# A fourth plain tile ahead of the seven-product tiles, spaced weight loads, and a gated half that stays in PSUM

## The reference

```python
def swiglu_ffn(h, wg, wu, wd):
    return (jax.nn.silu(h @ wg) * (h @ wu)) @ wd
...
    for i in range(DEPTH):
        kind, j = i % N_MIXERS, i // N_MIXERS
        sh1p, sc1p, g1p, sh2p, sc2p, g2p = adaln(c_prompt, ada_w[i], ada_b[i])
...
        xp = layer_norm(ALPHA * xp + g1p * op, ln_mix_g[i], ln_mix_b[i])
...
        fp = swiglu_ffn(xp * (1 + sc2p) + sh2p, ffn_w_gate[i], ffn_w_up[i], ffn_w_down[i])
...
        xp = layer_norm(ALPHA * xp + g2p * fp, ln_ffn_g[i], ln_ffn_b[i])
```

## Time and profile before

| | |
|---|---|
| median of 3 runs | 3110.5 us (3109.71 to 3116.89) |
| the profiled execution | 3103.62 us, span 3101.8 us |
| TensorE busy | 2932.5 us (95%), 21172 matmuls |
| GpSimd, VectorE, ScalarE busy | 56%, 53%, 30% |
| mean granted TensorE clock | 0.98 |

### The profile page before, as it was taken

One profiled execution on the slowest core, in us unless ns is written; L12 is line 12 of the kernel. 1 busy time (PEld: TensorE's weight loads), 2 busy tenths in 40 slices (PEclk: granted clock), 3 DMA queues, 4 the chain that ended last, 5 costly groups with the idle time before them and its releaser, 6 DMA issues.

```text
span 3101.8 us, 53473 instructions
## 1 busy us (share of the span) xinstructions
PE 2932.5 (95%) x21172; PEld 2700.2 (87%) x21172; DVE 1653.5 (53%) x3161; ACT 934.4 (30%) x1825; POOL 1734.0 (56%) x1209
## 2 busy tenths in 40 slices
PE   6999989999999989999989998999999999899997
PEld 4799989999976879999986687999997999899997
DVE  3254684636554774635565547463553536846263
ACT  2220152414220442414234324241422211424141
POOL 2455456857666456767620154676764565468575
PEclk8999999999999999999999999999999999999999
DMA  6643333443345433444321433344422323222332
GB/s 239 224 116 86 119 114 98 136 130 102 99 122 159 151 120 97 162 126 160 94 64 56 115 122 104 109 151 130 157 74 83 102 85 93 62 82 82 87 92 72
DMA packets 450486, 354.85 MB, mean 114 GB/s; under 512 B 26120, under 2 KB 424832, under 8 KB 437933
## 3 DMA queue, kind: packets, MB, share of 16 engines
q1 hardware_dynamic: 435744, 324.79, 34.0%
q10 hardware_dynamic: 14493, 26.63, 2.9%
HBM read 337.86 MB, written 5.25 MB: 111 GB/s over the span
## 4 chain that ended last, share of the span: by engine, by line
PE 76%; DVE 10%; ACT 4%; DMA 2%; issue 2%; DVEq 2%; POOL 1%; ACTq 1%; POOLq 1%; SPq 1%
PE pb L1142 75%; DMA w_raw<-in_ffn_w_up 2%; DMA ada_first<-in_ada_w 1%; DVE part L2727 1%; ACT h_hi L2134 1%; ACT hf L2134 1%; DVE h_lo L2787 1%; DVE xa L2753 1%; DVE pb L2746 1%; DVE hf L2768 0%; DVE h_lo L2777 0%; PE pb L1978 0%; DVE a_lo L2594 0%; POOL a_lo L1048 0%; DVE part L2722 0%
## 5 line engine op out<-in xcount | busy, mean ns | idle before, releaser
L978 POOL TENSOR_SCALAR w_hi<-w_raw 128x1024 fp32r<-128x1024 f32 (+2 forms) x264 | 277.9, 1053 | 714.5 <-DMA w_raw<-in_gmlp_w_in 279.3
L981 POOL TENSOR_TENSOR w_lo<-w_raw,w_hi 128x1024 fp32r<-128x1024 f32 (+2 forms) x264 | 625.8, 2370 | 44.0 <-issue 44.0
L1142 PE MATMUL pb<-a_hi,w_hi 128*128 128x288 f32 x2176 | 601.7, 300 | 33.9 <-POOL w_hi L978 31.9
L1142 PE MATMUL pb<-a_lo,w_hi 128*128 128x288 f32 x2176 | 595.6, 297 | 0.0
L1142 PE MATMUL pb<-h_hi,w_hi 128*128 128x288 f32 x2064 | 548.7, 302 | 47.0 <-DVE pr L2939 19.4
L1142 PE MATMUL pb<-h_lo,w_hi 128*128 128x288 f32 x2064 | 528.7, 297 | 0.0
L1023 POOL TENSOR_TENSOR w_lo<-w_raw,w_hi 128x512 fp32r<-128x512 f32 x304 | 400.8, 1340 | 163.7 <-DVE s_raw L2979 106.6
L1142 PEld LDWEIGHTS pb<-a_hi,w_hi 128*128 128x128 f32 x2176 | 414.2, 190 | 42.1 <-issue 35.5
L1142 PEld LDWEIGHTS pb<-h_hi,w_hi 128*128 128x128 f32 x2064 | 382.8, 191 | 62.3 <-DVE pr L2939 20.4
L1142 PEld LDWEIGHTS pb<-a_lo,w_hi 128*128 128x128 f32 x2176 | 414.7, 191 | 0.7
L1142 PEld LDWEIGHTS pb<-h_lo,w_hi 128*128 128x128 f32 x2064 | 378.7, 191 | 0.0
(11 more groups left out here) (373 smaller groups left out, 4950.5 us busy)
## 6 DMA issues: line engine op xcount, KB each, us to landing
ada_w<-in_ada_w SPq DMA_DIRECT2D x80, 1024.0 KB, 8.9
w_raw<-in_ffn_w_gate SPq DMA_DIRECT2D x88, 512.0 KB, 3.9
w_raw<-in_ffn_w_up SPq DMA_DIRECT2D x88, 512.0 KB, 3.9
w_raw<-in_gmlp_w_in SPq DMA_DIRECT2D x64, 512.0 KB, 4.2
w_raw<-in_ffn_w_down SPq DMA_DIRECT2D x64, 512.0 KB, 5.0
w_raw<-in_gmlp_w_out SPq DMA_DIRECT2D x32, 512.0 KB, 4.9
w_raw<-in_ffn_w_down SPq DMA_DIRECT2D x32, 384.0 KB, 3.7
w_raw<-in_conv_w_pw SPq DMA_DIRECT2D x24, 512.0 KB, 4.2
```

Source lines behind the costliest of these rows:

```text
L978: nc.gpsimd.tensor_scalar(w_hi[:, s, 0:w], w_raw[:, s, 0:w], 1.0, 1.0, ALU.mult, ALU.mult).then_inc(split_hi, 1)
L981: nc.gpsimd.tensor_tensor(w_lo[:, s, 0:w], w_raw[:, s, 0:w], w_hi[:, s, 0:w].bitcast(F32), ALU.subtract).then_inc(split_lo, 1)
L1142: return nc.tensor.matmul(out, lhsT, rhs, start=start, stop=stop)
```

## The change

1. `PAIRED_FROM` goes from 3 to 4: in each layer tile 3 is a plain tile.
2. Loads of conditioning weights are spread (`ada_asked`): one or two more behind a tile instead of four at once, and some between the down projection's units.
3. Slots: after each group's `sums_end` the circle is ordered anew, the slots in the order in which they come free, with the sums' slot third.
4. On GpSimd the first two units of the down weights are split ahead of the last tile's `gated_lower`, and t4 is made ahead of the first paired tile's forms.
5. In the plain tiles (but for the h0 halves of tiles 0 and 1) `gated_in_bank` multiplies in the up product's own PSUM bank and makes both parts from there; only then is that bank given back. Two of them stand ahead of t3 now.
6. In paired tiles the h0 half stays in the bank of p4. ScalarE reads its high part there, VectorE makes its low part (`gated_lower` on VectorE), and gives the bank back. GpSimd makes only the h1 half's.

```diff
-PAIRED_FROM = 3
+GU = ((0, 6), (6, 8), (14, 8))
+PAIRED_FROM = 4
...
+def ada_asked(l, m):
+
+    if m <= 2:
+        return ADA1
+    done = [t for t in ada_groups(l)[0] if t <= m - 2]
+    if not done:
+        return ADA_FIRST + (0, 1, 2, 4)[min(m, 5) - 2]
+    last = max(done)
+    apart = any(last < first <= m for first, _ in GU)
+    return ada_used_by(l, m - 2) + (ADA1 if apart else min(ADA1, m - last))
...
                 self.held[SLOTS - 1] = ("after", (acc_ready, self.products))
+                self.order, self.at = self.pairs[:2] + [SLOTS - 1] + self.pairs[2:], 0
...
                             load_to(plan.mark[l, "m", m])
-                            ada_to(l + 1, ADA1 if m < 4 else ada_used_by(l + 1, m - 3) + ADA1)
+                            ada_to(l + 1, ada_asked(l + 1, m))
                         if n < 2:
+                            load_to(plan.mark[l, "d", n] - 4)
+                            ada_to(l + 1, ada_used_by(l + 1, m) + 2)
+                            load_to(plan.mark[l, "d", n] - 2)
+                            ada_to(l + 1, ada_used_by(l + 1, m) + ADA1)
                             load_to(plan.mark[l, "d", n])
...
             def gated_lower(m):
 
-                for h in (1, 0):
-                    pool.wait_ge(gated_hi, AH.up())
-                    nc.gpsimd.tensor_tensor(one(a_lo, m, half_cols(h)), pr[:, h, :],
-                                            one(a_hi, m, half_cols(h)).bitcast(F32), ALU.subtract
-                                            ).then_inc(a_ready, 1)
+                pool.wait_ge(gated_hi, 2 * AH.up() - 1)
+                nc.gpsimd.tensor_tensor(one(a_lo, m, half_cols(1)), pr[:, 1, :],
+                                        one(a_hi, m, half_cols(1)).bitcast(F32), ALU.subtract).then_inc(a_ready, 1)
...
+                    U.up(2 * len(ms))
+                    split_to(U.n + 2)
                     gated_lower(ms[-1] - GU[n][0])
-                    U.up(2 * len(ms))
...
                 for h in (1, 0):
-                    if h:
-                        act.wait_ge(pair_gated, FQ.n)
-                    else:
-                        act.wait_ge(acc_free, BANKS + G.n)
-                    fn(one(a_hi, m, half_cols(h)), pr[:, h, :], ACT.Copy).then_inc(gated_hi, 1)
+                    act.wait_ge(pair_gated, 2 * FQ.n - h)
+                    src = pr[:, 1, :] if h else pb[:, (G.n - 1) % BANKS, 0:HALF]
+                    fn(one(a_hi, m, half_cols(h)), src, ACT.Copy).then_inc(gated_hi, 1)
...
+            def gated_in_bank(m, h, q):
+                up = pb[:, (G.n + 1) % BANKS, 0:HALF]
+                dve.wait_ge(acc_ready, G.n + 2)
+                dve.wait_ge(sg_ready, SG.up())
+                v.tensor_tensor(up, up, sg[:, q, :], ALU.mult).then_inc(acc_free, 1)
+                dve.drain()
+                v.tensor_copy(one(a_hi, m, half_cols(h)), up)
+                dve.drain()
+                v.tensor_tensor(one(a_lo, m, half_cols(h)), up, one(a_hi, m, half_cols(h)).bitcast(F32),
+                                ALU.subtract)
+                dve.drain().then_inc(a_ready, 1)
+                dve.sem_inc(acc_free, 1)
+                G.up(2)
...
+            def gated_lower(m):
+
+                gated = pb[:, (G.n - 1) % BANKS, 0:HALF]
+                dve.wait_ge(gated_hi, 2 * FQ.n)
+                v.tensor_tensor(one(a_lo, m, half_cols(0)), gated, one(a_hi, m, half_cols(0)).bitcast(F32),
+                                ALU.subtract)
+                dve.drain().then_inc(a_ready, 1)
+                dve.sem_inc(acc_free, 1)
...
                 form_last(l, m)
-                if m != PAIRED_FROM:
-                    dve.wait_ge(a_ready, 8 + a_before(l) + 2 * m)
+                if m != ms[0]:
+                    gated_lower(m - 1 - first)
...
-                v.tensor_tensor(pr[:, 0, :], p4, c11, ALU.mult).then_inc(acc_free, 1)
+                v.tensor_tensor(p4, p4, c11, ALU.mult)
+                dve.drain().then_inc(pair_gated, 1)
```

More of the change, by code:

```diff
@@ L539, in __init__ @@
                 self.slot, self.prior, self.ordinal = [], [], []
-                self.held, self.last, self.whole = [None] * SLOTS, SLOTS - 1, 0
+                self.held, self.whole = [None] * SLOTS, 0
+                self.order, self.at, self.pairs = list(range(SLOTS)), 0, []
                 self.sums_free = {}
@@ L547, in unit @@
                 self.freed.append(None)
[L548 to L551, removed]
+                if paired and self.order[self.at % SLOTS] == SLOTS - 1:
+                    self.at += 1
+                s = self.order[self.at % SLOTS]
+                self.at += 1
+                if paired:
+                    self.pairs = (self.pairs + [s])[-4:]
                 self.slot.append(s)
@@ L694, in plan_ffn @@
                     plan.mark[l, "m", m] = len(plan.srcs)
-                    if m == 2:
+                    if m == PAIRED_FROM - 1:
                         plan.mark[l, "turned"] = plan.products - 2
@@ L1077, in ffn @@
                         pool.drain().then_inc(t4_made, 1)
+                    forms_early(l, ms[0], FQ.n)
                     for m in ms:
@@ L1607, in gate_up @@
                     first_halves(wait_h, 1, slots)
[L1608 to L1611, removed]
+                    for _ in range(2, PAIRED_FROM):
+                        s_a, s_b = take_units(2)
+                        for h in (1, 0):
+                            for s in (s_a, s_b):
+                                half_product(s, KT, h, (h_hi, h_lo))
                 for m in paired_tiles(n):
@@ L3021, in paired @@
                 dve.wait_ge(acc_ready, G.n + 4)
+                if m != PAIRED_FROM:
+                    dve.wait_ge(a_ready, 8 + a_before(l) + 2 * m)
                 v.tensor_tensor(u23, p7, u23, ALU.add)
@@ L3053, in gate_up @@
                     v.tensor_tensor(t1_raw[:], t1_raw[:], h_lo[:, 0:QK, half_cols(0)].bitcast(F32), ALU.subtract)
+                    dve.drain().then_inc(t_sum, 1)
+                    for m in range(2):
+                        gated_in_bank(m, 1, m)
                     v.tensor_tensor(t3_raw[:], hf[:, 1], hf[:, 0], ALU.subtract)
@@ L3058, in gate_up @@
                     ada_pairs(l + 1, ADA_FIRST * more)
-                    for m in range(2):
-                        gated(m, 1, m)
+                    gated_in_bank(2, 1, 0)
                     dve.wait_ge(t_hi, 4 * l + 1)
                     v.tensor_tensor(t1_lo[:], t1_raw[:], t1_hi[:].bitcast(F32), ALU.subtract).then_inc(t_lo_dve, 1)
+                    gated_in_bank(2, 0, 1)
                     form_sums(l, ms[0], FQ.n)
-                    gated(2, 1, 0)
+                    gated_in_bank(3, 1, 0)
                     dve.wait_ge(t_hi, 4 * l + 3)
@@ L3068, in gate_up @@
                     form_lows(l, FQ.n)
-                    gated(2, 0, 1)
+                    gated_in_bank(3, 0, 1)
                 for m in ms:
@@ L3074, in gate_up @@
                         ada_part()
+                gated_lower(ms[-1] - first)
             def gmlp_v(c0, w, tt):
```

36 lines of the change are left out of this document (20 added, 16 removed).

## The result

| | median us (range) | span | against before |
|---|---|---|---|
| before, 4 runs beside the change | 3110.53 (3109.71 to 3116.89) | 3101.8 | |
| the change, 4 runs | 3039.45 (3033.63 to 3039.76) | 3031.8 | 0.9763 [0.9745, 0.9780] |

The change saves 71 us, 2.4% by the ratio; 3032 us was predicted. Its profiled execution took 3033.63 us.

The account below looks back on a forecast made before the run. TensorE was taken to bound the kernel: matmuls at 0.133 us plus waits and low clock after them. -36.7 - 41 - 7 + 6.4 = -78.3 us from 3103.6 gives 3025.3, plus 6.9 for the median: 3032 us; eight-in-ten range 3005 to 3075.

Parts of the forecast that it names:

- ends and spaced loads: Group ends and conditioning loads: gain 41 us from earlier down weights plus 7 from loads no longer issued four at once.
- starts and the fourth plain tile: Lead-in to each layer's first paired tile: gain 36.7 us from shorter waits, less 6.4 for the added plain matmuls.
- the half in PSUM: Paired tiles, h0 half kept in p4's bank: priced zero if the 0.3 us slack holds; a gain for VectorE itself.
- the bank of p4 paces the paired tiles: Rival: p4's bank, freed x us beyond the slack, costs 60x over 60 paired tiles; 3128 us at x = 1.6; chance 0.07.
- The row that the prediction named as the mark of this rival: TensorE's waits for VectorE's gated_lower: some 60 entries would prove the slow rival of p4's bank.
- Ends: Ends of groups, TensorE waiting for down weights' high part: 46 us lost, 5 left, gain 41, bounds 18 to 46.
- the 6 that were given as the mark: Sign: TensorE's waits for GpSimd's high parts should fall from 31.9 us to under 6.
- The spaced loads: Conditioning loads issued ahead of weights: about 10 us lost to late weights, 3 kept, gain 7, bounds 0 to 10.
- Starts: Lead-in to each layer's first paired tile: 58.7 us lost, 5.5 a layer to remain, gain 36.7, bounds 9 to 58.7.
- The rival in which GpSimd bounds the starts: GpSimd's full list leaves 12.5 us per layer lost before the first paired tile: 3060 us; chance 0.19, in part or full.
- Fourth plain tile: Tile 3 plain in each layer: 96 matmuls in place of 84, +6.4 us; gives 12.8 us more before the first paired tile.
- The bank in the plain tiles: Gated halves made from PSUM: 0.45 us an operation, 1.6 us a half against 5.2 from SBUF beside GpSimd.

Follow-up runs that it names:

- e1: The changed kernel timed once more, nothing altered: 3037.44 us, ratio 0.9774 to the kernel before.
- e3: The change with only item 6 undone: in paired tiles both gated halves go to SBUF and GpSimd makes both low parts; 3023.18 us.
- e8: The kernel before with only spaced loads, the new slot order and down units split first; three plain tiles, gated values in SBUF: 3050.35 us.
- e5: The change with GpSimd's two down-weight splits moved back behind the last tile's gated_lower: 3066.92 us.
- e6: The change with only the new order of the slots taken away: 3054.34 us.
- e9: e3 with three plain tiles in place of four (PAIRED_FROM = 3), GpSimd's forms ahead of t4 and ScalarE's residuals placed otherwise: 3029.64 us.
- e11: e3 with GpSimd's forms of the first paired tile put back ahead of the making of t4: 3017.51 us.
- e4: The change with plain tiles' gate-up product sent to SBUF and both parts made from there, at the same place in VectorE's list: 3040.17 us.
- e2: The change with ScalarE copying the h0 half, which stays in PSUM, first; GpSimd's low part waits for both copies: 3026.21 us.

## Why the prediction was right, and where it was off

The forecast of 3032 us is 7 us off on 3039.5, and the saving of 78.3 us is 71. The kernels split the saving by the prediction's own terms (differences of savings, each uncertain by some 5 us; e1 against e3 is that of the medians):

| term | forecast | measured | from |
|---|---|---|---|
| ends and spaced loads | -48 | -59.0 | e8 |
| starts and the fourth plain tile | -36.7 + 6.4 = -30.3 | -26.0 | e3 against e8 |
| the half in PSUM | 0 | +14.3 | e1 against e3 |
| sum | -78.3 | -70.7 | e1 |

**The half in PSUM is the step that failed,** though within the mechanism that the rival described: the bank of p4 paces the paired tiles. Its price was 60x with a slack of 0.3 us taken off first; the measured x is 0.26 us a tile, far from the 1.3 that would have turned the sign. Two things ate the slack. The bank is free only some 0.27 us after VectorE's instruction has ended (1425.13 to 1425.40), a hand-over which "ends near 1451.3" did not count; and VectorE's product ahead of it takes 1.19 us in the mean where e3 has 0.75 and the kernel before 0.64, because it falls earlier into one of GpSimd's operations. "For VectorE itself it is a gain" was wrong as well: the 191.4 us in which it stood for GpSimd are 106.0 us in which it stands for ScalarE, and e3, which has the wait for GpSimd again, is the faster kernel. The row that the prediction named as the mark of this rival came up with 35 entries, for a smaller x than the one that it would need to be slower.

**Ends.** Right in mechanism. The waits for GpSimd's high parts are 0.5 us, under the 6 that were given as the mark, and the clock is back. The 5 us and 3 us left in as remains of the ends and loads were not there: 59.0 is all of the 56 that the forecast held removable, and 3 us within the error. Of the two halves the splits are worth 28 us (e5) and the slots 16 (e6). With the loads' 4 that makes 48 where e8 has 59; how much of the 11 us is error and how much overlap of the parts was not told apart. The spaced loads are worth 4 of the forecast's 7, with 6.2 us of waits to show for it, but their ranges overlap.

**Starts.** 5.5 us a layer were to remain; 5.9 do, so by the stretches 58.7 - 4 x 5.9 = 35.1 us are gained where 36.7 were forecast (by the kernels 26.0 + 6.4 = 32.4). The parts in layer 1: the first bank 1.25 us (forecast 1.1), the low part of tile 2's weights 1.00 (1.6), the first form of GpSimd 0.40 (2.0), and the rest 0.67 + 1.76 (0.8). So the total is right by luck, with one error that offsets another: GpSimd's form was nearly in time, and the sum on VectorE that GpSimd holds for 2.77 us was not foreseen. The rival in which GpSimd bounds the starts did not come about. But e9 shows how near it was: with one plain tile less, it costs 3.6 us in each layer, and part of the clock behind it.

**Fourth plain tile.** Its +6.4 us are sure by count, and its cover was not priced apart. Between e9 and e11 it is worth 12 us net, so some 18 gross. Since e9 also has ScalarE's residuals at other places, that is for the tile with the order that goes with it.

**The bank in the plain tiles.** Costed right at 0.46 us an operation; its effect on the time is below what was measured (e4).

What stays open: why e2 is 3 us behind e3. The difference is within the error, but the paired tiles account for it, 711.9 us against 706.5; what holds them there was not followed up. That item 6 alone, in the kernel before, would cost as much was not tried.

## What to carry to other kernels

Before a result is left in a PSUM bank, write down the chain that frees the bank, with the hand-over of each semaphore and the order of the reader's list, and set it against the time at which TensorE wants the bank back. Here relief for an engine that only stood idle was worth nothing against it. When an engine's list gets shorter or is reordered, look again at every two-input SBUF operation of VectorE: how much is left of GpSimd's instruction when it starts decided here whether it took 0.7 or 2.8 us. And split a change into its items by undoing each: here one of six took a sixth of the gain back.

## What the runs showed of the hardware

- VectorE's cast of 288 float32 columns takes 458 ns from PSUM (all 24 of the change between 456 and 458), and its least from SBUF before the change is 310 ns. The rule weighed in the prediction (the Trainium skill, VectorE: DVE Perf Modes, section "Why PSUM operands drop a tier") put the difference at 0.14 us; it is 0.15. Beside GpSimd it is the other way round: the mean of the same cast from SBUF in e4 is 659 ns.
- VectorE's sum of 512 columns with two SBUF operands takes between 687 and 3084 ns in the change, with a median of 692.
- VectorE's product of 288 columns with two SBUF operands takes 0.46 to 0.47 us at the least. Started with more than 0.3 us left of a GpSimd operation, it ends 0.30 to 0.32 us after that operation does, in the change, in e2 and in e3.
- From the end of the VectorE instruction ahead of a bank's release to the start of the matmul that waits for it, 0.27 us pass (1425.13 to 1425.40 in the change, and the same at each of the 35 waits).
